# Turned residual scaled and rounded on ScalarE from its PSUM bank, its low part made from the bank too, and three small moves around it

## What is computed

```python
h = h + 0.5 * rms_norm(swiglu(rms_norm(h, g[0]), ffn_w13[i, 0], ffn_w2[i, 0]), g[1])
hn = rms_norm(h, g[2])
m = mixer(hn, ...)            # gmlp, rwkv7, dilated attention or gqa, by the layer
h = h + rms_norm(m, g[3])
h = h + 0.5 * rms_norm(swiglu(rms_norm(h, g[4]), ffn_w13[i, 1], ffn_w2[i, 1]), g[5])
gate = jax.nn.sigmoid(rms_norm(h, g[6]) @ ple_w_gate[i])
h = h + rms_norm(gate * (p[i] @ ple_w_proj[i]), g[7])
```

## Time and profile before

| what | value |
|---|---|
| median of 3 runs | 2274.13 us (2273.31 to 2275.44) |
| profiled execution, device time | 2272.61 us |
| its span, first to last instruction | 2270.8 us |
| TensorE busy | 2236.9 us (99%) |
| VectorE busy | 1467.1 us (65%) |
| ScalarE busy | 1154.9 us (51%) |
| GpSimd busy | 180.8 us (8%) |
| chain that ended last | PE 94%, DVE 3%, ACT 1%, issue 1% |
| mean granted TensorE clock | 0.999 |

### The profile page before, as it was taken

How to read it: one execution, slowest core, us unless ns; L and a number is a source line. 1 busy time by engine, 2 the same in 40 slices (tenths; PEclk the granted TensorE clock), 3 DMA queues, 4 the chain that set the end, 5 groups by cost and what they waited for, 6 DMA issues and landing times.

```text
span 2270.8 us, 33812 instructions
## 1 busy us (share of the span) xinstructions
PE 2236.9 (99%) x13395; PEld 1820.5 (80%) x13395; DVE 1467.1 (65%) x2079; ACT 1154.9 (51%) x1668; POOL 180.8 (8%) x286
## 2 busy tenths in 40 slices
PE   8999999999999999999999999999999999999998
PEld 6888888888888758878887888878888788868887
DVE  6656757656765877576567656656656765677655
ACT  5445545445544454254455445455445544565444
POOL 1001001001000010420011001001001100051001
PEclk9999999999999999999999999999999999999999
DMA  7556655554655640065556555524555555526553
GB/s 260 183 190 204 230 171 192 186 184 167 213 185 187 203 158 12 8 221 184 185 175 200 185 186 194 189 96 156 184 188 190 187 185 185 194 78 199 185 177 111
DMA packets 290091, 395.61 MB, mean 174 GB/s; under 512 B 11752, under 2 KB 193328, under 8 KB 289936
## 3 DMA queue, kind: packets, MB, share of 16 engines
q1 hardware_dynamic: 285072, 377.20, 50.3%
q0 software_dynamic: 4720, 16.20, 2.1%
q10 hardware_dynamic: 144, 0.07, 0.0%
HBM read 392.37 MB, written 1.05 MB: 173 GB/s over the span
## 4 chain that ended last, share of the span: by engine, by line
PE 94%; DVE 3%; ACT 1%; issue 1%; POOL 0%; DMA 0%; DVEq 0%; POOLq 0%; SPq 0%; ACTq 0%
PE bank L516 28%; PE bank L518 27%; PE bank L517 27%; PE bank L542 2%; PE bank L530 1%; PE bank L2560 0%; PE bank L2554 0%; ACT wh L637 0%; PE bank L1451 0%; ACT JUNK L644 0%; PE bank L2571 0%; PE bank L1966 0%; PE bank L1188 0%; DVE H L890 0%; PE bank L2531 0%
## 5 line engine op out<-in xcount | busy, mean ns | idle before, releaser
L823 DVE TENSOR_TENSOR wl<-raw,wh 128x1024 fp32r<-128x1024 f32 x708 | 859.0, 1223 | 554.8 <-ACT wh L637 554.4
L637 ACT ACTIVATE wh<-raw 128x1024 fp32r<-128x1024 f32 x708 | 744.2, 1058 | 648.1 <-PE bank L518 622.5
L516 PE MATMUL bank<-wh,XH 128*128 128x512 f32 x2000 | 801.0, 400 | 5.2 <-DVE wl L823 2.9
L518 PE MATMUL bank<-wh,XL 128*128 128x512 f32 x2000 | 780.7, 390 | 0.0
L517 PE MATMUL bank<-wl,XH 128*128 128x512 f32 x2000 | 780.5, 390 | 0.0
L516 PEld LDWEIGHTS bank<-wh,XH 128*128 128x128 f32 x2000 | 375.9, 188 | 94.5 <-issue 17.1
L518 PEld LDWEIGHTS bank<-wh,XL 128*128 128x128 f32 x2000 | 375.9, 188 | 81.6
L517 PEld LDWEIGHTS bank<-wl,XH 128*128 128x128 f32 x2000 | 376.5, 188 | 72.1 <-issue 0.5
L516 PE MATMUL bank<-wh,AH 128*128 128x512 f32 x704 | 276.0, 392 | 0.0
L518 PE MATMUL bank<-wh,AL 128*128 128x512 f32 x704 | 274.2, 389 | 0.0
L517 PE MATMUL bank<-wl,AH 128*128 128x512 f32 x704 | 274.1, 389 | 0.0
(11 more groups left out here) (339 smaller groups left out, 1725.3 us busy)
## 6 DMA issues: line engine op xcount, KB each, us to landing
raw<-in_ffn_w_dram SPq DMA_DIRECT2D x182, 512.0 KB, 4.7
raw<-in_ffn_wi_dram SPq DMA_DIRECT2D x176, 512.0 KB, 4.7
raw<-in_ffn_w_dram SPq DMA_DIRECT2D x40, 1024.0 KB, 4.9
raw<-in_ffn_wo_dram SPq DMA_DIRECT2D x40, 1024.0 KB, 4.8
raw<-in_a_wqkv_dram SPq DMA_DIRECT2D x18, 1024.0 KB, 4.8
raw<-in_a_w_in_dram SPq DMA_DIRECT2D x16, 1024.0 KB, 5.2
raw<-in_b_w_in_dram SPq DMA_DIRECT2D x12, 1024.0 KB, 4.9
bc<-in_norm_g_dram POOLq DMA_DIRECT2D x16, 512.0 KB, 5.2
```

What stands on the lines that cost most here:

```text
L516: pe.e.matmul(o, a, h, start=(k == 0), stop=False)
L518: m = pe.e.matmul(o, b, h, start=False, stop=(k == layer.nk - 1))
L637: act.e.activation(self.wh[j % N_W][:, 0:p.size], self.raw[p.chunk % N_RAW][:, p.at:p.at + p.size], ACT.Copy).then_inc(*self.rounded.up(j))
L823: dve.e.tensor_tensor(self.wl[j % N_W][:, 0:p.size], self.raw[p.chunk % N_RAW][:, p.at:p.at + p.size], self.wh[j % N_W][:, 0:p.size].bitca ...
```

## The change

- `dve_x_scale` and the scratch tiles `CT` are gone. ScalarE makes `XH` from the turned bank with four instructions of 128x128 for each half, each with its own gain column as the scale.
- VectorE makes `XL` from the bank, the gain column and `XH` with four instructions of 128x128 for each half, `bank * gain - XH`. It waits for the last of the four `XH` of that half. `dve_x` is low, low.
- TensorE waits for `XH` and `XL` feature slice by feature slice (k) and no more by halves; a turn bank is free when the last `XL` of its half is made.
- `pe_turn_own` turns tile 1 in steps 8 and 9 where the stage before is ple or dilated (into 4, 8, 12 and 10).
- `dve_out` weights the first output block of both tiles ahead of the `leave` of the block's last part, not after it.
- In the scan the second group of idle matmuls moves from unit (1, 0) to unit (1, 1).

```diff
     def pe_turn_x(self, pe, n, t, b):
 
-        bank = self.turn_bank(pe, ("x", n, t, b), (self.x_scaled, n, t, b))
+        bank = self.turn_bank(pe, ("x", n, t, b), (self.x_lo, n, t, 4 * b + 3))
...
     def x_ready(self, n):
-        return lambda k, t: [(self.x_hi, n, t, k // 4), (self.x_lo, n, t, k // 4)]
+        return lambda k, t: [(self.x_hi, n, t, k), (self.x_lo, n, t, k)]
...
     def pe_turn_own(self, pe, n, step):
 
-        first = 6 if n else 2
+        first = 2 if n == 0 else 8 if STAGES[n - 1][0] in ("ple", "dilated") else 6
...
+    def x_parts(self, n, t, k):
+
+        block, c = self.gains(n)
+        turned = self.bank(self.place["turn", ("x", n, t, k // 4)])[:, (k % 4) * P:(k % 4 + 1) * P]
+        to = [x[:, k, t * P:(t + 1) * P] for x in (self.XH, self.XL)]
+        if STAGES[n][0] == "dilated":
+            turned = turned.rearrange("p (b c) -> p c b", c=4)
+            to = [x.rearrange("p (c b) -> p c b", c=4) for x in to]
+        return turned, self.GT[:, block, c + k:c + k + 1], *to
+
     def act_x_hi(self, act, n, t, b):
-        act.wait_ge(self.x_scaled, n, t, b)
-        act.e.activation(self.XH[:, 4 * b:4 * b + 4, t * P:(t + 1) * P], self.CT[b][:, :, :], ACT.Copy).then_inc(
-            *self.x_hi.up(n, t, b))
+        act.wait_ge(self.consts, "gains" if self.gains(n)[0] == 0 else "gains2")
+        act.wait_ge(self.turned, "x", n, t, b)
+        for k in range(4 * b, 4 * b + 4):
+            turned, gain, hi, _ = self.x_parts(n, t, k)
+            act.e.activation(hi, turned, ACT.Copy, scale=gain).then_inc(*self.x_hi.up(n, t, k))
...
+    def dve_x_lo(self, dve, n, t, b):
+        dve.wait_ge(self.consts, "gains" if self.gains(n)[0] == 0 else "gains2")
         dve.wait_ge(self.turned, "x", n, t, b)
...
-    def dve_x_lo(self, dve, n, t, b):
-        hi, lo = (x[:, 4 * b:4 * b + 4, t * P:(t + 1) * P] for x in (self.XH, self.XL))
-        dve.wait_ge(self.x_hi, n, t, b)
-        dve.e.tensor_tensor(lo, self.CT[b][:, :, :], hi.bitcast(F32), ALU.subtract).then_inc(*self.x_lo.up(n, t, b))
+        dve.wait_ge(self.x_hi, n, t, 4 * b + 3)
+        for k in range(4 * b, 4 * b + 4):
+            turned, gain, hi, lo = self.x_parts(n, t, k)
+            dve.e.scalar_tensor_tensor(lo, turned, gain, hi.bitcast(F32), ALU.mult, ALU.subtract).then_inc(
+                *self.x_lo.up(n, t, k))
...
     def dve_x(self, dve, n, t):
-        for b in range(2):
-            self.dve_x_scale(dve, n, t, b)
         for b in range(2):
             self.dve_x_lo(dve, n, t, b)
...
             if i == half - 1:
-                self.leave(dve, p.j + N_W)
                 for t in range(T):
                     self.dve_weigh(dve, n, 0, t, self.pair((n, "out", 0))[t])
+                self.leave(dve, p.j + N_W)
...
     def pe_scan_krv(self, pe, t, o):
         banks = self.scan_pair(pe, ("krv", t, o), (self.moved, "rh", t, o, 1))
-        if (t, o) in ((0, 1), (1, 0)):
+        if o == 1:
             self.pe_keep(pe, banks[0], 6 - t)
```

More of the change, by code:

```diff
@@ L311, in __init__ @@
         self.AL = at("AL", EO + FF // P * S * 4, [P, FF // P, S], F32R)
-        self.CT = [at(f"CT{i}", EO + 54784 + 2048 * i, [P, 4, P], F32) for i in range(2)]
         self.gU = at("gU", EO + 32768, [P, T, 2048], F32)
@@ L417, in __init__ @@
         self.used = [count(f"used{t}") for t in range(T)]
-        self.turned, self.x_scaled, self.x_hi, self.x_lo = (
-            count(x) for x in ("turned", "x_scaled", "x_hi", "x_lo"))
+        self.turned, self.x_hi, self.x_lo = (count(x) for x in ("turned", "x_hi", "x_lo"))
         self.squared, self.rs = count("squared"), count("rs")
@@ L824, in leave @@
                             self.wh[j % N_W][:, 0:p.size].bitcast(F32), ALU.subtract).then_inc(*self.left.up(j))
[L826 to L830, removed]
-        dve.wait_ge(self.turned, "x", n, t, b)
[L832 to L841, removed]
-    def dve_x_lo(self, dve, n, t, b):
-        hi, lo = (x[:, 4 * b:4 * b + 4, t * P:(t + 1) * P] for x in (self.XH, self.XL))
-        dve.wait_ge(self.x_hi, n, t, b)
-        dve.e.tensor_tensor(lo, self.CT[b][:, :, :], hi.bitcast(F32), ALU.subtract).then_inc(*self.x_lo.up(n, t, b))
+    def dve_x_lo(self, dve, n, t, b):
+        dve.wait_ge(self.consts, "gains" if self.gains(n)[0] == 0 else "gains2")
+        dve.wait_ge(self.turned, "x", n, t, b)
+        dve.wait_ge(self.x_hi, n, t, 4 * b + 3)
[3 more added lines that the diff above has]
+                *self.x_lo.up(n, t, k))
     def dve_x(self, dve, n, t):
-        for b in range(2):
-            self.dve_x_scale(dve, n, t, b)
         for b in range(2):
@@ L926, in dve_start @@
         dve.e.memset(self.NEG[:, :], -0.5).then_inc(*self.neg.up())
-        for b in range(2):
-            self.dve_x_scale(dve, 0, 0, b)
         self.dve_x_lo(dve, 0, 0, 0)
```

## The result

The changed kernel takes **2284.03 us** at the median (2283.12 to 2284.93, 5 runs), beside 2274.13 us (2273.31 to 2282.99, 5 runs) for the kernel before in the same comparison. The ratio is **1.0039, 95% interval 1.0026 to 1.0052**: slower by 9 to 10 us, beyond the 0.2% that can be told from no change. The forecast was slower by 3.2 us (2277.3), and the measured time lies 1 us above the range's high end. The profiled execution took 2284.07 us, its span is 2282.3 us, and its mean granted TensorE clock is 0.996, where that of before was 0.999.

A forecast was written before the change was run, and what follows sets the result against it. TensorE, busy 99% of the span, was taken as the bound, with step 7 at joins released by VectorE's chain. Terms +2.95, +3.3, +0.95, -1.65, -1.2, -1.2 gave +3.2 us, so 2277.3 us; range 2270 to 2283.

The forecast's parts named there:

- ScalarE's spacing: Narrow `XH` on ScalarE: starts every 0.25 us, from pairs of widths 512 and 256; bounds 0.18 and 0.36 us.
- D: Delay of VectorE's chain at a join through the narrow instructions: 0.7 us, with bounds 0.2 and 1.5.
- Rival (a): Thirteen joins: narrow instructions cost the skill page's 0.29 us or more, D 1.0, +7.1 us, 2281.2 us; chance 0.20.
- Rival (c): Narrow instructions overlap well: spacing 0.18 us, D 0.2, 2271.9 us; with D at 0, -4.1 us, 2270.0; chance 0.20.
- Rival (b): The two small gains, weighting and idle matmuls, don't come: +5.6 us, 2279.7 us; chance 0.12.
- Six joins: Joins into stages that start with `XH`: step 7 moves by D less slack, +2.95 us.
- Out of ple: Three joins out of ple: release moves by D and both turns come behind it, +3.3 us.
- Into ple: Four joins into ple: the turn in step 6 has slack 0.46 us against D, +0.95 us.
- Dilated: Join out of dilated: the 1.4 us wait in step 6 goes and the first step gains 0.25 us, -1.65 us.
- Weighting: Rwkv stage: two weightings fit into VectorE's idle time ahead of the `leave`, -1.2 us; elsewhere nothing.
- Idle matmuls: Scan: the moved group fits where TensorE idles 1.22 us at unit (1, 1), -1.2 us, 0 at worst.
- Tile 1's narrow instructions, waits by slice: Tile 1's `XH` and `XL` are covered by eight matmul steps, and slice waits cost nothing: both counted at nothing.

The follow-up runs named there:

- moves_only: Kernel before, wide instructions kept, with the dilated join's tile 1 turned late, weighting ahead of the `leave` and idle matmuls moved: 2270.00 us, ratio 0.9981.
- narrow_leave: Kernel before with the narrow `XH` and `XL`, and VectorE's first `leave` put ahead of tile 0's `XL`: 2274.93 us, ratio 0.9998.
- after_ple_early: Changed kernel with tile 1 turned in steps 6 and 7 again behind ple: 2278.49 us, ratio 1.0016.
- narrow_only: Kernel before with only the narrow `XH` and `XL` and their waits by slice: 2288.28 us, ratio 1.0057.
- after_again: Changed kernel run once more, without an edit: 2282.65 us.
- leave_keep_old: Changed kernel, first `leave` ahead of tile 0's `XL`, tile 1 turned in steps 7 and 8 except behind ple and dilated, idle matmuls put back: 2268.31 us.

## Why the prediction was right or wrong

**The direction, the bound and the chain were right.** TensorE's waits at the joins decide, step 7 is held by the last `leave` of VectorE's chain, and narrow instructions move it. The eviction in the gap, which leaves all narrow instructions and takes only one `leave` out of the chain, gives 6.3 of the 7.7 us back.

**Sizes.** ScalarE's spacing: 0.255 us, forecast 0.25. The line through the widths 512 and 256 held down to 128. The figures of the Trainium skill, page *ScalarE: Activation LUTs*, section "What ACT_TABLE_LOAD costs", give an estimate of 0.29 us from start to start, and the trace differs: its four start 0.255 us apart. D came out at 0.79 us at the ordinary joins and 0.83 us behind ple, not at 0.7: the fourth `XH` lasts 375 and not 350 ns, and VectorE starts 0.09 us behind its end. Rival (a)'s condition, D from 0.8, was reached by that and not by its own mechanism, a wider spacing. Rival (c) is out by the same 0.255 us; its case of D = 0 was also summed wrongly, since the late turns out of ple cost 3 x 0.4 us at any D, so it gives -2.85 us and not -4.1. Rival (b) is out since both small gains came, 1.20 and 1.34 us in `moves_only`.

**Six joins**: +3.3, forecast +2.95. The parts were off in opposite ways. Into stage 1 it is 0.4 and not 0.7 us: in the profile of before the residual of tile 1 there, released by GpSimd's power, starts 5.36 us behind the start of tile 0's turn, where the other joins have 4.99, a slack of 0.37 us that I had not seen. The five others lost 0.57 and not 0.45 us.

**Out of ple**: D and the extra turn came as forecast, 1.25 us a join and not 1.1 us. **The step that failed is what stands behind that wait.** I wrote that a single wait of over 2.5 us would show in step 7, put its length into the sum, and counted nothing for TensorE having no work that long. Two of three joins paid 1.6 us more, at a granted clock of 0.50 for 3.4 us.

**Into ple**: +1.2, forecast +0.95; the turn had a slack of 0.48 us against D's 0.79. **Dilated**: -1.66, forecast -1.65, and the first turn has no wait above 0.2 us:

```profile
1563.87 0.39 PE L515 MATMUL bank<-wh,XL 128*128 128x512 f32 x1
1564.18 0.66 PE L527 MATMUL bank<-ident,H 128*128 128x128 f32 x4
```

**Weighting**: -1.2 as forecast; TensorE's extra wait ahead of the turn is 990.91 - 990.31 - 0.227 = 0.37 us:

```profile
990.31 0.39 PE L515 MATMUL bank<-wh,XL 128*128 128x512 f32 x1
990.91 0.66 PE L527 MATMUL bank<-ident,H 128*128 128x128 f32 x4 [0.22 <-DVE H L884]
```

**Idle matmuls**: the gap at unit (1, 1) is closed (they end and the product starts at once, 918.12 to 919.43), -1.39 us against -1.2. The scan as a whole lost 2.1 us in the profiled run: its tail at half clock cost 2.5 us, and the short waits ahead of it 1.0 us.

```profile
918.12 1.38 PE L473 MATMUL bank<-ident 128*128 128x128 f32 x10
919.43 0.97 PE L2536 MATMUL bank<-rV,sKR 64*64 64x64 f32 x26
```

**Tile 1's narrow instructions, waits by slice**: nothing, as forecast: behind step 7 of a join the matmuls of both traces keep their distance, and `narrow_leave`, which has them all, is level with before.

**The sum**: +3.2 forecast, +3.7 measured once the clock is kept. The missing 5 to 6 us are for the most part a term that the sum did not have. The rivals had none either: each of them varied the length of waits, and none asked what TensorE's clock does when waits are joined into one. The range was too narrow for that reason and not for the bounds of the spacing.

## What to carry to other kernels

Making an engine's step shorter or longer is worth what the chain behind it says, and a gap that an edit opens on the engine that holds the chain is where the held instruction should go: the same narrow instructions cost 7.7 or 1.4 us, by the place of one subtraction at each join. Two waits of TensorE that an edit merges into one cost more than their sum once the clock falls behind it; put the turn between them, or idle matmuls into the wait. And look at TensorE's busy time with an equal count of instructions before looking at waits: if it grew, read the granted clock of short windows first, since the 40 slices of the profile's page show 9 throughout.

## What the runs showed of the hardware that I had not expected

- At the ple joins, behind a stretch of 2.70 to 2.78 us in which TensorE had no work, the granted clock fell to 1.2 GHz for 3.4 us at six of nine such places (two of three in each of three profiles, not always the same ones); with the stretch filled by idle matmuls at none of six, and at none of nine where the longest wait at the join was 1.5 to 1.6 us (`after_ple_early`, `narrow_only`, `narrow_leave`). One fall cost 1.6 us.
- In the scan it fell without a long wait, behind a wait of 0.2 to 0.4 us and one of 0.95 us among matmuls of 64 columns, in three of seven profiles with the idle group moved and unfilled, in none of five with the group at its old place and in neither of two with the turns filled. Two waits of these sizes stand in `after_again`, before and `leave_keep_old` too, without a fall. One such fall cost 2.5 us. That is too few to call either the cause.
- Apart from this, 17 of 88 runs of the kernel before had a clock of 0.994 to 0.996 and took some 8 us more, and so had some runs of every other version. The one profiled run of before did not fall into it, so where that stretch lies and what brings it stays open.
- Back to back, `XH` instructions out of PSUM with a column as their scale start 0.255 us apart on ScalarE at 128 columns, and VectorE's 128x128 operation with a column costs 343 ns from a bank as from SBUF.
